# The second tile's attention projections moved into the head of a four-phase trunk kernel, and odd routing phases that start with the pair already loaded

## The reference

```
for i in range(DEPTH):                      # 2
    xn = rmsnorm(h, mixer_norm[i])
    h = h + swa_attention(xn, ...)          # i = 0;  hgrn2(xn, ...) for i = 1
    h = h + peer_ffn(rmsnorm(h, ffn_norm[i]), w_q, sub_keys, u_tab, v_tab)
return rmsnorm(h, final_norm)

# peer_ffn, for a row x and each of its 8 x 16 experts e:
act = gelu(dot(x, u_tab[e]))
y += gate[e] * act * v_tab[e]
```

## Time and profile before

| | |
|---|---|
| median of 3 runs | 1596.5 us (1595.95 to 1601.55) |
| the profiled execution's own time | 1599.69 us |
| its span | 1597.7 us |
| PE, DVE, ACT, POOL busy | 87%, 67%, 42%, 35% of the span |
| DMA | 644.25 MB, mean 403 GB/s |
| mean granted TensorE clock | 0.973 of full |

### The profile page before, as it was taken

How to read it: one execution, slowest core, us unless ns; L and a number is a source line. 1 busy time by engine, 2 the same in 40 slices (tenths; PEclk the granted TensorE clock), 3 DMA queues, 4 the chain that set the end, 5 groups by cost and what they waited for, 6 DMA issues and landing times.

```text
span 1597.7 us, 15793 instructions
## 1 busy us (share of the span) xinstructions
PE 1382.7 (87%) x4912; PEld 745.8 (47%) x4912; DVE 1065.3 (67%) x2556; ACT 667.9 (42%) x1903; POOL 562.0 (35%) x518
## 2 busy tenths in 40 slices
PE   8759989888879989998888999999898888977776
PEld 4545545443436656554343665656443443422222
DVE  2278576765667676778576667678868575667644
ACT  2233443455343433544535244254454433344333
POOL 0033334334334322334433333233443433444431
PEclk9879999999999999999999999999999998999999
DMA  9389999999999999999999999999999999999995
GB/s 385 146 329 424 422 421 422 422 421 417 422 422 423 422 422 366 420 423 420 421 422 420 423 422 423 350 424 420 390 422 421 422 423 422 421 422 421 422 422 249
DMA packets 85491, 644.25 MB, mean 403 GB/s; under 512 B 9760, under 2 KB 10400, under 8 KB 13728
## 3 DMA queue, kind: packets, MB, share of 16 engines
q0 software_dynamic: 73728, 536.90, 81.2%
q1 hardware_dynamic: 11248, 106.12, 15.9%
q10 hardware_dynamic: 432, 0.24, 0.0%
HBM read 642.17 MB, written 1.05 MB: 403 GB/s over the span
## 4 chain that ended last, share of the span: by engine, by line
PE 43%; DMA 32%; DVE 15%; ACT 9%; issue 2%; SPq 0%; DVEq 0%; ACTq 0%
DMA ring<-experts,idx 31%; PE acc L1192 25%; DVE ring L875 7%; PE rbank L1163 5%; PE ab L1106 2%; PE ab L1110 2%; ACT L508 2%; PE y L991 2%; ACT diag L401 1%; PE y L1155 1%; PE ab L980 1%; ACT coef L401 1%; ACT gel L508 1%; PE cbank L1122 1%; PE acc L980 1%
## 5 line engine op out<-in xcount | busy, mean ns | idle before, releaser
L1192 PE MATMUL acc<-ring,diag 128*128 128x512 f32 x2048 | 995.0, 614 | 178.4 <-ACT diag L401 171.1
L391 POOL DMA_INDIRECT ring<-experts,idx x512 | 560.8, 1095 | 1008.2 <-PE acc L1192 896.8
L875 DVE CUSTOM_DVE_ANT_0 ring<-ring,xn 128x1024 f32<-128x1024 f32 x512 | 624.6, 1223 | 316.4 <-DMA ring<-experts,idx 310.4
L1192 PEld LDWEIGHTS acc<-ring,diag 128*128 128x128 f32 x2048 | 364.0, 193 | 619.1 <-ACT diag L401 333.4
L508 ACT ACTIVATE gel<-dots 128x1 f32<-128x1 f32 x512 | 103.5, 202 | 775.5 <-DVE dots L875 774.7
L401 ACT ACTIVATE diag<-ident,coef 128x128 f32<-128x128 f32 x512 | 205.7, 402 | 16.7
L401 ACT ACTIVATE coef<-gate,gel 128x1 f32<-128x1 f32 x512 | 150.9, 295 | 16.6
L1163 PEld LDWEIGHTS rbank<-xTs,wroute 128*128 128x128 f32 x896 | 120.7, 199 | 57.4 <-issue 48.2
L1163 PE MATMUL rbank<-xTs,wroute 128*128 128x128 f32 x896 | 121.5, 282 | 9.9 <-DMA wroute<-route_w 9.0
L1106 PEld LDWEIGHTS ab<-xTs,wmix 128*128 128x128 f32 x512 | 64.0, 192 | 10.5 <-issue 10.5
L1106 PE MATMUL ab<-xTs,wmix 128*128 128x128 f32 x512 | 67.6, 275 | 0.0
(11 more groups left out here) (187 smaller groups left out, 941.3 us busy)
## 6 DMA issues: line engine op xcount, KB each, us to landing
wroute<-route_w SPq DMA_DIRECT2D x16, 2304.0 KB, 12.7
wmix<-hgrn_in SPq DMA_DIRECT2D x16, 2048.0 KB, 12.0
ring<-experts,idx POOLq DMA_INDIRECT x512, 15.3
wmix<-hgrn_out SPq DMA_DIRECT2D x8, 1024.0 KB, 11.9
ring<-attn_in SPq DMA_DIRECT2D x4, 1536.0 KB, 14.4
wmix<-attn_out SPq DMA_DIRECT2D x6, 1024.0 KB, 15.3
wmix<-attn_in SPq DMA_DIRECT2D x4, 1536.0 KB, 12.2
gain<-gains SPq DMA_DIRECT2D x5, 512.0 KB, 8.8
```

Of the source, the lines that this page charges most:

```text
L391: pool.indirect_dma_start(out=ring[:, k * 2 * D:(k + 1) * 2 * D], out_offset=None, in_=experts, in_offset=bass.IndirectOffsetOnAxis(ap=idx ...
L875: dve.tensor_tensor_reduce(out=u_rows(k), in0=u_rows(k), in1=xn[:, tile], scale=1.0, scalar=0.0, op0=ALU.mult, op1=ALU.add, accum_out=dots ...
L1192: last = nc.tensor.matmul(acc[:, j * HALF:(j + 1) * HALF], diag[:, n % DIAGS], v_rows(k)[:, j * HALF:(j + 1) * HALF], start=n % PER == 0, ...
```

## The change

Tile 1 is loaded, normed and transposed in the head as well, and its transposed copy is kept in a third side of `xTs`. After tile 0's attention, `ahead(g, ks)` projects tile 1 with the same weights `win0(g)`, still in the ring, into `acc`, and ScalarE copies each result to `stash(g)` in `wmix`, from where phase 0 rotates it. The four loads of attn_in and the four of attn_out for tile 1 are gone; `wout0(g)` all lie in `wmix` and are used twice. The ring's slots 0 to 5 are freed group by group (`ring_groups`), 6 and 7 are free from the start, and the slot of gather n becomes (n + 6) % 8. In phase 0 attention starts at position -6 with a period of 16, and the first loads of the recurrence's weights are issued at 37 and 69.

Odd phases route the pairs in the order 3, 0, 1, 2, so that the first finds its weights in `wroute`: the loads at position 50 of phases 0 and 2 are gone. The gains of the mixers are multiplied in after the transpose, as numbers by partition (`gained`), instead of in the norm before it; three broadcast gains remain. The dummy matmuls are 7 instead of 4, the first weight load is split in two, and SP waits for landings between the loads of the head.

```diff
-ATTN_PERIOD = 20
+ATTN_HEAD = -6
+ATTN_PERIOD = 16
@@
+        def stash(g):
+            return wmix[:, g // 2, 4 * D + g % 2 * AW:4 * D + (g % 2 + 1) * AW]
+        def slot_of(n):
+            return (n + 6) % RING
+        def pair_at(p, at_):
+            return at_ if p % 2 == 0 else (3, 0, 1, 2)[at_]
+        def route_loads(p, at_):
+            return 7 * (p // 2) + (at_ + 1 if p % 2 == 0 else 4 + at_)
+        def ring_groups(k):
+            return (1, 2, 2, 3, 4, 4)[k]
@@ sync
-            load_gain(0, 0, 0)
-            sp.dma_start(win0(0), attn_in[0]).then_inc(wattn0_in[0], 16)
+            half = AIN // 2
+            sp.dma_start(win0(0)[:, 0:half], attn_in[0][:, 0:half]).then_inc(wattn0_in[0], 16)
+            sp.dma_start(win0(0)[:, half:AIN], attn_in[0][:, half:AIN]).then_inc(wattn0_rest, 16)
+            sp.dma_start(h[:, 1], x[1]).then_inc(x1_in, 16)
+            sp.wait_ge(x0_in, 16)
             sp.dma_start(win0(1), attn_in[1]).then_inc(wattn0_in[1], 16)
+            sp.wait_ge(wattn0_rest, 16)
             sp.dma_start(win0(2), attn_in[2]).then_inc(wattn0_in[2], 16)
...
-            load_attn_in(0)
-            load_attn_out(0)
-            load_attn_in(1)
-            load_attn_out(1)
             load_route(0, 1)
...
-                    elif q == 50 and p < 3:
+                    elif q == 50 and p == 1:
                         load_route(p + 1, 0)
@@ gpsimd
-                if n == 0:
-                    pool.wait_ge(a_outproj, ITERS)
+                if n < RING and k < 6:
+                    pool.wait_ge(a_proj, ITERS + ring_groups(k))
@@ scalar
+            def stash_qkv(g):
+                act.wait_ge(a_proj, ITERS + g + 1)
+                copy(stash(g), acc[:, g % 2 * HALF:g % 2 * HALF + AW]).then_inc(a_stash, 1)
...
             for unit in range(2):
                 route_copy(-1, unit)
+            stash_qkv(0)
             for unit in range(2):
                 route_exp(-1, unit)
+            for g in range(1, ITERS):
+                stash_qkv(g)
@@ vector
+            def norm_plain(k, tile):
+                dve.wait_ge(rstd_ready, k + 1)
+                dve.tensor_scalar(xn[:, tile], h[:, tile], rstd[:], None, ALU.mult).then_inc(norm_done, 1)
+            def gained(k, side, layer, half, source):
+                dve.wait_ge(xT_ps, 2 * k + half + 1)
+                ks = slice(4 * half, 4 * half + 4)
+                dve.tensor_tensor(xTs[:, side, ks], source.rearrange("p (k t) -> p k t", k=4),
+                                  gainT[:, layer, ks].unsqueeze(2).broadcast_to([P, 4, P]), ALU.mult).then_inc(xT_mix, 1)
@@ tensor
+            def ahead(g, ks):
+                if ks[0] == 0:
+                    if g == 0:
+                        pe.wait_ge(xT_mix, 4)
+                        pe.wait_ge(a_rope, ITERS)
+                    elif g >= 2:
+                        pe.wait_ge(a_stash, g - 1)
+                project_qkv(acc[:, g % 2 * HALF:(g % 2 + 1) * HALF], 2, win0(g), ks)
...
-            for _ in range(4):
+            for _ in range(7):
                 nc.tensor.matmul(rbank[:], prob[:, 0:P], prob[:, 0:HALF], start=True, stop=True)
...
             out0(3)
-            transposes(1, 0, 0)
-            transposes(1, 0, 1)
+            ahead(0, range(0, 6))
+            transposes(2, 0, 0, ab[:, 0])
+            transposes(2, 0, 1, ab[:, 1])
             route_begin(0)
             for c in range(2):
                 route_project(0, c, range(KT))
             route_scores(0)
             for c in range(2, 4):
                 route_project(1, c, range(KT))
+            ahead(0, range(6, KT))
             route_scores(1)
+            for g in range(1, ITERS):
+                ahead(g, range(KT))
```

More of the change, by code:

```diff
@@ L287, in load_hgrn_in @@
                 if n < 2:
-                    sp.wait_ge(a_outproj, 2 * ITERS - 1 + j)
+                    sp.wait_ge(a_outproj, ITERS + 2 + 2 * j)
                 else:
@@ L297, in load_hgrn_out, with load_route, load_gain @@
                 sp.dma_start(wmix[:, :, HIN:5 * D], hgrn_out[i]).then_inc(whgrn_out_in, 16)
[L299 to L304, removed]
+            def load_route(p, at_):
+                if p or at_:
+                    sp.wait_ge(r_score, p * UNITS + (0, 2, 3, 4)[at_])
+                sp.dma_start(wroute[:], route_w[(p // 2) * ITERS + pair_at(p, at_)]).then_inc(wroute_in, 16)
+            def load_gain(row, after):
                 if after:
                     sp.wait_ge(norm_done, after)
-                sp.dma_start(gain[:, slot], gains[row:row + 1].to_broadcast([P, D])).then_inc(gain_in[slot], 16)
+                sp.dma_start(gain[:], gains[row:row + 1].to_broadcast([P, D])).then_inc(gain_in, 16)
             def hgrn_loads(p, q):
@@ L609, in norm_ims, with norm_scale @@
                 dve.reciprocal(ims[:], ms[:]).then_inc(ims_ready, 1)
-            def norm_scale(k, tile, slot, loads):
-                dve.wait_ge(gain_in[slot], 16 * loads)
+            def norm_scale(k, tile, loads):
+                dve.wait_ge(gain_in, 16 * loads)
                 dve.wait_ge(rstd_ready, k + 1)
-                dve.scalar_tensor_tensor(xn[:, tile], h[:, tile], rstd[:], gain[:, slot], ALU.mult, ALU.mult).then_inc(norm_done, 1)
+                dve.scalar_tensor_tensor(xn[:, tile], h[:, tile], rstd[:], gain[:], ALU.mult, ALU.mult).then_inc(norm_done, 1)
+            def norm_plain(k, tile):
[6 more added lines that the diff above has]
+                                  gainT[:, layer, ks].unsqueeze(2).broadcast_to([P, 4, P]), ALU.mult).then_inc(xT_mix, 1)
             def norm_xT(k, side):
@@ L623, in rotate @@
             def rotate(n, tile, bank):
-                dve.wait_ge(a_v, n + 1)
+                if tile == 0:
+                    dve.wait_ge(a_v, n + 1)
+                else:
+                    dve.wait_ge(a_stash, n - ITERS + 1)
                 qk = bands(bank[:, 0:QK], GQ + 1)
@@ L882, in beside @@
                     add_up(tile, acc[:])
-                elif q == 3:
+                elif q == 3 and p:
                     norm_ims(norm_at(p, 0))
[L885 to L888, removed]
+                elif q == 4 and p == 3:
+                    norm_scale(norm_at(p, 0), tile, 3)
+                elif q == 4 and p:
+                    norm_plain(norm_at(p, 0), tile)
+                elif q in (6, 7) and p in (1, 2):
+                    gained(norm_at(p, 0), 0, 1, q - 6, ab[:, q - 6])
                 if p == 0 and q == 90:
@@ L925, in _ @@
             norm_ims(0)
-            norm_scale(0, 0, 0, 1)
-            norm_xT(0, 0)
+            norm_plain(0, 0)
+            dve.wait_ge(gainT_in, 16)
+            gained(0, 0, 0, 0, ab[:, 0])
+            gained(0, 0, 0, 1, ab[:, 1])
+            norm_ims(1)
+            norm_plain(1, 1)
             dve.wait_ge(rope_in, 16 * len(ROPE))
             rope0(0)
+            gained(1, 2, 0, 0, y[:, 0:HALF])
+            gained(1, 2, 0, 1, y[:, HALF:D])
             dve.wait_ge(early_in, 16 * len(EARLY))
@@ L965, in _, with transposes @@
             norm_ims(norm_at(3, 1))
-            norm_scale(norm_at(3, 1), 1, 0, 3)
+            norm_scale(norm_at(3, 1), 1, 3)
         @block.tensor
         def _(pe):
-            def transposes(k, tile, half):
+            def transposes(k, tile, half, to):
                 if half == 0:
@@ L974, in transposes, with project_qkv @@
                     at_ = (half * 4 + c) * P
-                    last = nc.tensor.transpose(ab[:, half, c * P:(c + 1) * P], xn[:, tile, at_:at_ + P], ident[:])
+                    last = nc.tensor.transpose(to[:, c * P:(c + 1) * P], xn[:, tile, at_:at_ + P], ident[:])
                 last.then_inc(xT_ps, 1)
-            def project_qkv(to, w, ks):
+            def project_qkv(to, side, w, ks):
                 for k in ks:
-                    last = nc.tensor.matmul(to[:, 0:AW], xTs[:, 0, k], w[:, k * AW:(k + 1) * AW], start=k == 0, stop=k == KT - 1)
+                    last = nc.tensor.matmul(to[:, 0:AW], xTs[:, side, k], w[:, k * AW:(k + 1) * AW], start=k == 0, stop=k == KT - 1)
                 if ks[-1] == KT - 1:
@@ L1049, in attention @@
                 w = 192
[L1050 to L1059, removed]
+                if r == 10:
                     transpose_qk(n, ab[:, 1])
@@ L1219, in beside @@
                 if q in (MIXED + 4, MIXED + 5):
-                    transposes(norm_at(p, 1), tile, q - MIXED - 4)
+                    transposes(norm_at(p, 1), tile, q - MIXED - 4, ab[:, q - MIXED - 4])
                 for unit in range(2):
```

138 lines of the change are left out of this document (58 added, 80 removed).

## The result

The changed kernel takes 1583.16 us (median of 4 runs, 1580.28 to 1584.05); the kernel before took 1596.3 (4 runs). The ratio is 0.9907 with a 95% interval of 0.9883 to 0.9931: faster, by 13 us and not by 27. The prediction's range, 1560 to 1580, doesn't hold it.

A forecast was written before the change was run, and what follows sets the result against it. Transfers were taken to bound phase 0, engines mid phase 2, with a serial head. Gains of 6.5 + 18.5 + 1.5 = 26.5 us, about 27, took 1599.7 to 1572.7, or 1569.5 on the median's scale; range 1560 to 1580.

The forecast's parts named there:

- Phase 0, the step that failed: Phase 0: 8.13 MB of loads removed, 19.3 us by bytes, of which 18.5 us was taken as gain.
- Rival C: Phase 0 becomes engine-bound where packed attention meets route units 3 and 4; 12 us or fewer of 19.3; chance 0.11.
- The route load in phase 2: Phase 2: dropping the 2.359 MB load at 1039.59 us, where engines bind, was taken to gain 1.5 us.
- Rival B: Phase 2: the dropped load at 1039.59 us counts in full by bytes; 1565.5 us; chance 0.12.
- the move that I had costed at nothing: Phase 2: the load of gain row 4 moves inside the phase, costed at nothing.
- The head: Before the first gather: group 1 begins 2.7 us earlier and a filled PE wait saves 3.8 us; 6.5 us in all.
- The second part: Head, after out0(3): ahead(0) steps fill PE's 4.51 us wait, keeping the clock up; 3.8 us gained.
- Rival A: Head: the clock stays low, costing 6.6 us of the gain; 1576 us; chance 0.13.
- rival D: Hand-over after the head: late ahead(3) on a half-clock PE lets transfers run dry; 1589 us; chance 0.04.
- rival E: Phase 0: the change doesn't remove the bytes it claims, loads still issued; 1590 us; chance 0.02.
- the few tenths that I added for the first norm: Added to the 26.5 us sum for the first norm, making 27 us.
- The scale: Sum set against the profiled 1599.7 us, giving 1572.7, then put on the median's scale, 3.2 us lower: 1569.5.

The follow-up runs named there:

- warm4: The changed kernel with 4 dummy matmuls in place of 7; 1580.93 us, ratio 0.9884 to the kernel before.
- before2: The kernel before, run once more unchanged for a second trace; 1599.85 us, span 1598.0.

## Why the prediction was wrong, step by step

The forecast was 1569.5, the median 1583.16: 13.7 us. They divide so.

**Phase 0, the step that failed: 5.9 us.** I wrote that "VectorE's 44.2 us of waiting is over twice what goes", and took 18.5 of the 19.3 us. It gave 12.6, near the 12 that I had as the lower bound. The waiting was real, and after the change there is nearly as much of it (57.3 us for 63.3), but the argument compared sums over 293 us, while the slack has to lie where the work is. Period 16 takes attention's waits and VectorE steps out of the last third of phase 0 and packs them onto routing's steps; there the path ran over attention's hand-overs, and the last 155 us were bound by transfers with 46.9 us of waits that nothing could use. The two experiments on start and period show that the period is the cause; with period 20 phase 0 is 18.6 us shorter than before, so the price by bytes was right. Rival C named the mechanism and gave 12 us or fewer of the 19.3; its sign, a DMA share under 0.95 in phase 0, is there (0.87 from 260 to 280 us); I had it at 0.11. A check was at hand, the waits by stretch beside the new positions of the steps; whether it would have given 12.6 isn't known. Which of the steps meet (exponentials with two table loads at position 57, behind the pair selection of units 3 and 4 at 51 to 56) is only read from the timeline. The clock, at 0.74 from 260 to 280 us, isn't needed for the dip: warm4 has 344 GB/s in the same stretch at 0.91, and start 8 with period 16 has 344 GB/s at 1.00. Whether it made this one deeper stays open.

**The route load in phase 2: 1.5 us expected, none seen.** The direction of this step was right: engines bind there, and 2.36 MB fewer buy nothing. POOL's timelines of before and of the changed kernel, gathers 312 and 360, show it. Gather 312 is the last before the load that was dropped (1039.59 us), and the distance is 18.73 us at both:

```profile
1038.94 0.93 POOL L391 DMA_INDIRECT ring<-experts,idx  x1 [2.10 <-PE acc L1192]
...
1177.62 0.94 POOL L391 DMA_INDIRECT ring<-experts,idx  x1 [0.50 <-PE acc L1192]
```

```profile
1020.21 0.94 POOL L386 DMA_INDIRECT ring<-experts,idx  x1 [2.09 <-PE acc L1212]
...
1158.89 0.94 POOL L386 DMA_INDIRECT ring<-experts,idx  x1 [0.50 <-PE acc L1212]
```

Rival B is refuted. Behind gather 128 the distance goes from 18.7 to 17.1 us, 1.6 us more for the miss, in three small steps. In phase 1, 1.2 us are lost (396.8 us against 395.6); but the second trace of before has 397.1 there, so this is no more than executions differ by. The other two lie at the gain of row 4. Before loads it at 877 us, and between gathers 264 and 312 the change wins 1.3 us; the changed kernel loads it at 1163 us, and between gathers 376 and 384 it loses 1.6. Gathers 360 to 384 take 62.5 us in both traces of before and 63.5 to 65.1 in every kernel with the change. So the move that I had costed at nothing took and gave about the same; that it is the cause wasn't tried. Together with the 1.5 the 1.6 make 3.1 us.

**The head: right, 6.1 for 6.5 us.** Group 1 began at 18.19 for 17.8, ahead(3) ended at 97.2 for 97.3, the first slot came free at 102.3 for 101.9, gather 0 at 85.4 for 85.0. Two parts of the reasoning don't stand. The second part was sized from one execution: the clock's return varies, and without the filling its price was 2.4 us for the 3.8 counted, and a second trace of before has its head 2.3 us shorter. And the 7 dummy matmuls aren't needed for the clock: with 4 the projection is as fast, and the 7 delay the transposes, from 7.31 to 10.59 us. They also ended 1.1 us later than the 9.5 that I worked out, since the first six of their records were slow where it had been three before; smaller terms that came out short left 0.4 us of this at group 1. And set against the second trace of before the head gives 3.8 us, so that it came near 6.5 is in part the luck of which execution was traced. Rival A (clock low in the head) is refuted by the rows above, rival D (hand-over) by the DMA share of 0.99 and 1.01 around it, and rival E by the 16.2 MB that are gone. With the few tenths that I added for the first norm, the head makes 0.9 us of the miss.

**The scale: 3.7 us.** The sum was rightly made against the profiled 1599.7, but then I took off the 3.2 us by which this stood above three runs. The changed kernel's profiled execution stands 0.5 under its median. Seven to nine later runs of before put its median at 1598 to 1599, so the offset was that of the first three runs. 5.9, 3.1, 0.9 and 3.7 make 13.6.

This division holds for the first trace of before. Against the second, phase 0 misses 5.3 us, the head 3.2 and what lies behind gather 128 1.0. So only the part of phase 0 is settled in its size.

## What to carry to other kernels

Slack must be counted where the work will lie: when a change both frees transfers and moves engine work, set the new positions of the steps against the waits by stretch, not against their sum. Bytes taken out of a stream are worth their time only where an engine waits for them; the same 2.36 MB cost 5.6 us or nothing here, and the wait of the consumer told which. The offset between a profiled execution and a median of three runs was smaller here (3.2 us) than the spread of the runs (5.6 us), so it belongs in the range and not in the sum. Small steps of 1 or 2 us between two traces need a second trace of the same kernel before they are given a cause.

## What the runs showed of the hardware

Behind 4 or 7 dummy matmuls TensorE's clock stayed at 2.4 GHz (granted 1.00) through gaps of 0.42 and 0.53 us and eight transposes. It fell to 1.2 GHz within an idle time of 4.5 us (granted 0.50 after it), and it came back at different moments: the same 32 records of the route projection took 6.68, 6.16 and 5.33 us after such a gap, 3.81 without it. At the start of the kernel, too, it came up at different moments: by the spacing of the dummy matmuls' records, 0.86 us and then 0.43, it was up by 5.0, 5.3, 6.0 and 7.6 us in four traces (before, before2, warm4, changed), though the granted clock of a window shows 1.00 there from the start. Transposes follow the clock as matmuls do (1.97 us for eight records against 1.04 to 1.09).
